# Routing of two expert mixtures in another order: loads, shift, masks, slots and ranking

## What is computed

```python
p_group = jax.nn.softmax((t @ w_rg + b_rg).astype(jnp.float32), axis=-1)
grp = jnp.argmax(p_group, axis=-1)
...
top_p, top_i = lax.top_k(jax.nn.softmax(logits_in, axis=-1), TOP_K)
top_p = top_p / jnp.sum(top_p, axis=-1, keepdims=True) * p_g
```

## Time and profile before

| what | value |
|---|---|
| timed runs | 1819.88, 1822.99, 1823.16 us; median 1822.99 |
| the profiled execution | 1820.98 us, its span 1819.2 us |
| busy in the span | TensorE 1633.8 us (90%), VectorE 553.0 us (30%), ScalarE 322.6 us (18%), POOL 174.0 us (10%) |
| chain that ended last | TensorE 70%, DMA 16%, VectorE 9% |
| first routing | norm's last sum ends at 779.05 us, first gather on TensorE at 808.54 us |
| second routing | last sum ends at 1272.7 us, first gather at 1296.86 us |

### The profile page before, as it was taken

The page is one execution under the profiler, slowest core; times in us unless marked ns, Lnnn a source line. Parts: engine busy times, 40 slices in busy tenths (PEclk is TensorE's granted clock), DMA queues, the critical chain, the costliest instruction groups (busy, mean ns, idle before and its releaser), DMA issues.

```text
span 1819.2 us, 21572 instructions
## 1 busy us (share of the span) xinstructions
PE 1633.8 (90%) x8392; PEld 1057.2 (58%) x8392; DVE 553.0 (30%) x1120; ACT 322.6 (18%) x648; POOL 174.0 (10%) x180
## 2 busy tenths in 40 slices
PE   5799999999999989969998789988799998999985
PEld 1466666776588868855554369757534543443433
DVE  2266666666520011153122110382511111011002
ACT  2223333333231100011001021241100000000001
POOL 1144333334300000000000000000000000000000
PEclk8799999999999978969999899899699999999999
DMA  9311110111834413418999974103299989999993
GB/s 392 145 52 46 35 46 27 43 46 35 337 114 162 142 67 123 147 54 349 421 421 420 421 278 161 48 1 120 88 409 422 395 349 422 421 359 387 421 422 158
DMA packets 59644, 404.91 MB, mean 223 GB/s; under 512 B 6782, under 2 KB 7938, under 8 KB 13232
## 3 DMA queue, kind: packets, MB, share of 16 engines
q1 hardware_dynamic: 53328, 381.92, 52.7%
q0 software_dynamic: 6240, 21.92, 4.0%
HBM read 402.71 MB, written 1.10 MB: 222 GB/s over the span
## 4 chain that ended last, share of the span: by engine, by line
PE 70%; DMA 16%; DVE 9%; issue 2%; ACT 1%; SPq 0%; DVEq 0%; POOL 0%; POOLq 0%; ACTq 0%
PE bank L601 69%; DMA ring<-in_moe 14%; DVE arena L1619 2%; DMA ring<-in_dense 2%; ACT arena L1261 1%; DVE arena L1650 1%; DVE arena L1666 1%; PE bank L1017 1%; DVE arena L1655 0%; DVE arena L1647 0%; DVE arena L1645 0%; DVE arena L1659 0%; DMA arena<-in_router_w 0%; DMA arena<-decay_rows 0%; DVE arena L1669 0%
## 5 line engine op out<-in xcount | busy, mean ns | idle before, releaser
L601 PE MATMUL bank<-ring,arena 128*64 128x512 f32 (+2 forms) x2304 | 521.5, 606 | 58.6 <-DMA ring<-in_moe 56.9
L601 PE MATMUL bank<-arena 128*128 128x128 f32 (+3 forms) x2864 | 426.5, 300 | 35.2 <-DVE arena L1949 14.6
L601 PEld LDWEIGHTS bank<-arena 128*128 128x128 f32 (+2 forms) x2864 | 379.0, 194 | 134.0 <-ACT arena L1261 47.8
L601 PEld LDWEIGHTS bank<-ring,arena 128*64 128x64 f32 (+2 forms) x2304 | 174.6, 138 | 369.9 <-issue 364.9
L1261 ACT ACTIVATE arena<-bank 128x256 f32<-128x256 f32 (+1 forms) x369 | 164.1, 451 | 1186.0 <-PE bank L601 892.1
L601 PE MATMUL bank<-hc,head_w 128*128 128x512 f32 (+1 forms) x384 | 166.3, 541 | 3.0 <-DMA head_w<-in_head_w 3.0
L1971 DVE TENSOR_TENSOR arena<-arena,bank 128x256 f32<-128x256 f32 x48 | 20.2, 422 | 360.7 <-ACT arena L1261 360.7
L601 PE MATMUL bank<-arena,ring 128*128 128x256 f32 x512 | 116.6, 388 | 4.3 <-ACT arena L1261 2.6
L601 PEld LDWEIGHTS bank<-arena,ring 128*128 128x128 f32 x512 | 99.7, 195 | 19.7 <-ACT arena L1261 3.4
L601 PE MATMUL bank<-hc,ring 128*128 128x256 f32 x512 | 110.7, 380 | 0.0
L601 PEld LDWEIGHTS bank<-hc,ring 128*128 128x128 f32 x512 | 97.5, 190 | 12.9
(11 more groups left out here) (241 smaller groups left out, 1056.7 us busy)
## 6 DMA issues: line engine op xcount, KB each, us to landing
ring<-in_moe SPq DMA_DIRECT2D x288, 1024.0 KB, 13.2
ring<-in_dense SPq DMA_DIRECT2D x72, 1024.0 KB, 7.0
head_w<-in_head_w POOLq DMA_DIRECT2D x27, 512.0 KB, 4.0
arena<-decay_rows POOLq DMA_DIRECT2D x16, 256.0 KB, 4.6
xc<-in_xc SPq DMA_DIRECT2D x1, 2048.0 KB, 8.6
arena<-bias_rows POOLq DMA_DIRECT2D x2, 1024.0 KB, 8.5
mats<-in_square SPq DMA_DIRECT2D x1, 1088.0 KB, 11.6
out_y<-xc SPq DMA_DIRECT2D x2, 512.0 KB, 2.9
```

Of the source, the lines that this page charges most:

```text
L601: return nc.tensor.matmul(out, lhsT, rhs_, start=start, stop=stop, **kw)
```

## The change

Both routings are changed in the same way:

- The router's weights and `attn` are loaded when the first of the eight residual tiles is there, not the last.
- VectorE only scales the tiles (one scalar-tensor-tensor each, with gain and norm), and ScalarE adds the shift (`shift`, an Identity with a bias column). TensorE adds the logits' bias first, not last; in the second routing this waits for the first shifted tile.
- The masks of the first and second choice that `route1` and `route2` already have are used for the slots; the gates' search for them goes. In the second routing `keep` is the sum of two masks, each multiplied by the chosen group.
- Slots are computed twice. `place_fixed` gives the fixed experts their slots, and all others a base of 4096, which no unit holds. The first gathers (two in the first mixture, one in the second) are made from it. Then the ranking runs, and `place_ranked` adds the ranked experts' bases, less 4096, and computes slots again. Counting and ordering come ahead of that in the first mixture, and last in the second.
- Constant tables (`make_tables`) are made before the logits come.

The diff, cut to its core (eight columns of indentation taken off where the code is inside `build`):

```diff
+FAR = 4096.0
...
-second = area(12480, QT, E1)
...
+base_fixed = area(16656, E1)
...
-    pool.wait_ge(s["residual"], KT)
+    pool.wait_ge(s["residual"], 1)
     pool.dma_start(arena[:, 10752:10752 + KT * (GROUPS1 + E1 + E2)], t["router_w"]).then_inc(s["router_landed"], 16)
     pool.dma_start(hw[:, 0:1024 + 4 * P], t["attn"]).then_inc(s["attn_landed"], 16)
...
-    pool.wait_ge(s["residual"], 3 * KT)
+    pool.wait_ge(s["residual"], 2 * KT + 1)
...
         logits = [bank[5][:, qt * width:(qt + 1) * width] for qt in range(QT)]
+        at = D + (0, GROUPS1 + E1)[m]
+        if m == 1:
+            pe.wait_ge(s["route_in"], KT + 1)
+        for qt in range(QT):
+            mm(logits[qt], ones[0:1, :], one_row[0:1, 0, at:at + width], qt == 0, False, skip_group_check=True)
         for k in range(KT):
-            pe.wait_ge(s[f"route_in{m}"], k + 1)
+            pe.wait_ge(s["route_in"], KT * m + k + 1)
             for qt in range(QT):
-                mm(logits[qt], src[:, k, qt * P:(qt + 1) * P], router_w[m][:, k, :], k == 0 and qt == 0, False,
-                   skip_group_check=True)
-        at = D + (0, GROUPS1 + E1)[m]
-        for qt in range(QT):
-            ins = mm(logits[qt], ones[0:1, :], one_row[0:1, 0, at:at + width], False, qt == QT - 1, skip_group_check=True)
+                ins = mm(logits[qt], src[:, k, qt * P:(qt + 1) * P], router_w[m][:, k, :], False,
+                         k == KT - 1 and qt == QT - 1, skip_group_check=True)
         ins.then_inc(s["logits_made"], 1)
...
+    def shift(m):
+        into = H if m == 0 else X
+        for k in range(KT):
+            by = mod[:, 3 * KT + k, 0:1] if m == 0 else V("ln1_b")[:, k:k + 1]
+            act.wait_ge(s["route_scaled"], KT * m + k + 1)
+            act_fn(into[:, k, :], into[:, k, :], ACT.Identity, bias=by).then_inc(s["route_in"], 1)
     def route(m, experts):
+        shift(m)
...
         ins = stt(X[:, j, :], bank[j % 4][:, 0:SEQ], mod[:, 2 * KT + j, 0:1], X[:, j, :], ALU.mult, ALU.add)
         ins.then_inc(s["residual"], 1)
     dve.wait_ge(s["rnorm"], 1)
-    for half in range(2):
-        ks_ = range(half * KT // 2, (half + 1) * KT // 2)
-        link(tt_(H[:, ks_[0]:ks_[-1] + 1, :], X[:, ks_[0]:ks_[-1] + 1, :], times(norm_r, len(ks_)), ALU.mult))
-        for k in ks_:
-            ts_(H[:, k, :], H[:, k, :], ffns[:, k:k + 1], mod[:, 3 * KT + k, 0:1], ALU.mult, ALU.add
-                ).then_inc(s["route_in0"], 1)
+    for k in range(KT):
+        stt(H[:, k, :], X[:, k, :], ffns[:, k:k + 1], norm_r, ALU.mult, ALU.mult).then_inc(s["route_scaled"], 1)
...
         return tt_(out, out, over(pick_m[:, 0:rows], c), ALU.is_equal)
-    def make_falling():
+    starts = rs[9]
+    def make_tables(m):
+        experts, first = (E1, E2)[m], FIXED[m]
         dve.wait_ge(s["attn_landed"], 16)
         link(ts_(falling, slot_numbers[:, 0:E1], -1.0, float(P), ALU.mult, ALU.add))
+        link(ts_(base_fixed[:, 0:first], slot_numbers[:, 0:first], float(CAP), None, ALU.mult))
+        link(nc.vector.memset(base_fixed[:, first:experts], FAR))
+        link(nc.vector.memset(base[:, 0:first], 0.0))
+        link(ts_(starts[:, 0:UNITS[m]], slot_numbers[:, 0:UNITS[m]], float(P), None, ALU.mult))
...
+            link(ts_(base[:, first:experts], free_[:, 0:n], float(CAP // 2), CAP * first - FAR, ALU.mult, ALU.add))
...
+            link(ts_(base[:, first:experts], free_[:, 0:n], float(CAP), CAP * first - FAR, ALU.mult, ALU.add))
...
-    def place_tokens(m, kept, gates):
+    def find_slots(m, first, second):
         experts = (E1, E2)[m]
-        first = rt[8][:, 0:QT * experts].rearrange("p (a b) -> p a b", a=QT)
-        prod = rt[9][:, 0:QT * experts].rearrange("p (a b) -> p a b", a=QT)
-        second_ = second[:, :, 0:experts]
-        top = rs[6][:, 0:QT]
-        link(red(choice_gates[:, 0, :], gates, AX_X, ALU.max))
-        link(first_largest(first, gates, choice_gates[:, 0, :], experts))
-        link(tt_(second_, kept, first, ALU.subtract))
-        link(tt_(prod, second_, gates, ALU.mult))
-        link(red(choice_gates[:, 1, :], prod, AX_X, ALU.add))
-        dve.wait_ge(s["placed"], m + 1)
+        prod = rt[8][:, 0:QT * experts].rearrange("p (a b) -> p a b", a=QT)
         place = position[:, :, 0:experts]
-        link(cp(counts_f[:, 0:experts], bank[6][:, 2 * experts:3 * experts]))
-        link(ts_(base[:, 0:FIXED[m]], slot_numbers[:, 0:FIXED[m]], float(CAP), None, ALU.mult))
-        link(cp(rt[0][:, 0:experts], counts_f[:, 0:experts]))
-        rank_experts(m, rt[0][:, 0:experts])
-        link(tt_(place, bank[6][:, 0:QT * experts].rearrange("p (a b) -> p a b", a=QT),
-                 times(base[:, 0:experts], QT), ALU.add))
         link(tt_(prod, place, first, ALU.mult))
         link(red(slot_of[:, 0:QT], prod, AX_X, ALU.add))
-        link(tt_(prod, place, second_, ALU.mult))
+        link(tt_(prod, place, second, ALU.mult))
         link(red(slot_of[:, QT:2 * QT], prod, AX_X, ALU.add))
-        starts = rs[9][:, 0:UNITS[m]]
-        link(ts_(starts, slot_numbers[:, 0:UNITS[m]], float(P), None, ALU.mult))
-        link(tt_(slot_in[:, :, 0:UNITS[m]], over(slot_of, UNITS[m]), times(starts, 2 * QT), ALU.subtract))
+        link(tt_(slot_in[:, :, 0:UNITS[m]], over(slot_of, UNITS[m]), times(starts[:, 0:UNITS[m]], 2 * QT), ALU.subtract))
+    def place_fixed(m, first, second):
+        experts = (E1, E2)[m]
+        dve.wait_ge(s["placed"], m + 1)
+        link(tt_(position[:, :, 0:experts], bank[6][:, 0:QT * experts].rearrange("p (a b) -> p a b", a=QT),
+                 times(base_fixed[:, 0:experts], QT), ALU.add))
+        link(cp(rt[0][:, 0:experts], bank[6][:, 2 * experts:3 * experts]))
+        find_slots(m, first, second)
+    def place_ranked(m, first, second):
+        experts = (E1, E2)[m]
+        place = position[:, :, 0:experts]
+        link(tt_(place, place, times(base[:, 0:experts], QT), ALU.add))
+        find_slots(m, first, second)
+    def choose_gates(m, second):
+        experts = (E1, E2)[m]
+        gates = gate_rows[:, :, 0:experts]
+        prod = rt[8][:, 0:QT * experts].rearrange("p (a b) -> p a b", a=QT)
+        link(red(choice_gates[:, 0, :], gates, AX_X, ALU.max))
+        link(tt_(prod, second, gates, ALU.mult))
+        link(red(choice_gates[:, 1, :], prod, AX_X, ALU.add))
...
+        link(cp(counts_f[:, 0:FIXED[m]], rt[0][:, 0:FIXED[m]]))
         link(red(top[:, 0:1], counts_f[:, 0:experts], AX_X, ALU.max))
         cp(most[:, :], top[:, 0:1]).then_inc(s["counted"], 1)
         order_experts(m)
...
-        place_tokens(0, keep[:, :, 0:E1], gate_rows[:, :, 0:E1])
+        place_fixed(0, top1, top2)
+        return top1, top2
...
-        link(tt_(w4, w4, top2, ALU.add))
         link(tt_(sm, m1, m2, ALU.add))
...
         link(tt_(w4, w4, over(hot, PER2), ALU.mult))
-        w3 = w.rearrange("p (a b) -> p a b", a=n)
-        cp(keep[:, :, 0:E2], w3).then_inc(s["kept"], 1)
+        link(tt_(top2, top2, over(hot, PER2), ALU.mult))
+        w3, top2_3 = (rt[i][:, 0:n * E2].rearrange("p (a b) -> p a b", a=n) for i in (3, 9))
+        tt_(keep[:, :, 0:E2], w3, top2_3, ALU.add).then_inc(s["kept"], 1)
         link(nc.vector.reciprocal(gm, gs))
         dve.wait_ge(s["kept"], 2)
-        link(tt_(w, w, ex, ALU.mult))
-        link(tt_(gate_rows[:, :, 0:E2], w3, over(gm, E2), ALU.mult))
-        place_tokens(1, keep[:, :, 0:E2], gate_rows[:, :, 0:E2])
-    def mixture(m):
+        link(tt_(ex3, ex3, keep[:, :, 0:E2], ALU.mult))
+        link(tt_(gate_rows[:, :, 0:E2], ex3, over(gm, E2), ALU.mult))
+        choose_gates(1, top2_3)
+        place_fixed(1, w3, top2_3)
+        return w3, top2_3
...
         make_gather(0)
+        if ahead == 2:
+            make_gather(1)
+        rank_experts(m, rt[0][:, 0:(E1, E2)[m]])
         copy_x(0)
-        make_gather(1)
+        if ahead == 2:
+            count_tokens(m)
+            choose_gates(m, second)
+        place_ranked(m, first, second)
+        if ahead == 1:
+            make_gather(1)
         for i, of in enumerate((slot_of, choice_gates.rearrange("p a b -> p (a b)"))):
             for j in range(2 * QT):
                 ins = ts_(slot_diag[:, 4 * i + j, :], M("ident"), of[:, j:j + 1], None, ALU.mult)
                 if i == 0 or j < 2 * QT - 1:
                     link(ins)
...
+            count_tokens(m)
         hidden(0)
...
+                stt(X[:, k, :], X[:, k, :], V(name + "_g")[:, k:k + 1], norm_r, ALU.mult, ALU.mult
+                    ).then_inc(s["route_scaled"], 1)
+            return
         for half in range(2):
             ks_ = range(half * KT // 2, (half + 1) * KT // 2)
             rows = X[:, ks_[0]:ks_[-1] + 1, :]
             link(tt_(rows, rows, times(norm_r, len(ks_)), ALU.mult))
```

More of the change, by code:

```diff
@@ L1858, in route1 @@
                 n = QT
-                make_falling()
+                make_tables(0)
                 dve.wait_ge(s["logits_made"], 1)
@@ L1989, in mixture @@
                 ins.then_inc(s["slots_spread"], 1)
```

(22 more changed lines are left out.)

5 lines of the change are left out of this document (2 added, 3 removed).

## The result

The changed kernel takes 1802.42 us (median of 5 runs, 1801.51 to 1808.37); beside it the kernel before took 1819.88 us (5 runs, 1816.44 to 1823.16). The ratio is 0.9917, its 95% interval 0.9896 to 0.9938: **0.83% faster**. The forecast was 1810 us, 0.65% off 1821.75. The five runs of before are the three that the forecast knew and two shorter ones, so their median fell from 1822.99 to 1819.88. The saving is thus 15.1 us by the ratio and 17.5 by the medians, where the sum had 11.8.

A forecast was written before the change was run, and what follows sets the result against it. Both expert mixtures were taken as bound by the weight stream, which stops during the routings. Gains of 3.1 + 5.3 + 0.7 + 2.65 = 11.8 us, taken from a mean of 1821.75, gave 1810 us, range 1803.5 to 1815.

The forecast's parts named there:

- Router weights in A, 3.1 us: First routing, up to the logits: earlier router start gains 2.13 us, bias moved into the pause 1.0; together 3.1 us.
- Logits to first gather, 5.3 and 2.65 us: Fixed slots ahead of the ranking start the first gather 5.3 us earlier in the first routing, 2.65 in the second.
- What lies in the gather's shadow: First routing: second gather and ranking, 4.7 us, hidden under TensorE's 6.75 us gather; slack 2.1, or 0.8 late at full clock.
- Slots, not the order: First mixture: the stream follows the release of slots, so it gains TensorE's shift of 8.4 us, not the restart's 12.
- About 856.5: First mixture, a sign: TensorE's first long wait for weights comes at about 856.5 us instead of 864.92.
- the restart at 815.2: First mixture: order at 811.3 us, plus 3.9 from order to moving weights, restarts the stream at 815.2.
- weights moving 4 us after the order: First mixture, a sign: the weight stream moves again 4 us after the ranked order is ready.
- No table load: ScalarE's Identity shifts cost no table load; the rival, chance 0.04, had 2 x 1.28 us more, 1812.6 us.
- the second routing's input, 0.7 us: Second routing: TensorE's router starts at 1274.88 instead of 1275.58 us; the bias stays in the chain; gain 0.7 us.
- the clock stays up: Rival, chance 0.20: shorter pauses keep TensorE's clock up, each routing's router passes gain up to 3.2 us more; 1803.6 us.
- the clock rises later: Rival, chance 0.07: the clock rises within `up` instead of before the gather's end, losing 3.5 us at most once; 1813.5 us.

The follow-up runs named there:

- late_loads: The changed kernel with the loads of router weights and table back at the last residual; 1806.16 us, ratio 0.9930.
- warm_more: The changed kernel with unread 256-column matmuls in TensorE's pauses of both routings (3, 4 and 7) and nine at the attention's start; 1795.12 us, ratio 0.9861; repeated 0.9852.
- order_late: The changed kernel with counting and ordering of the experts put back behind the diagonals in the first mixture; 1802.70 us, ratio 0.9920.
- inputs_only: The kernel before with the new input side alone (early loads, scaling and shift tile by tile, bias first); 1815.21 us, ratio 0.9977.
- masks_only: The kernel before with only the masks reused and the tables made earlier, the ranking still ahead of the first gather; 1813.51 us, ratio 0.9971.
- slots_only: The changed kernel with the input side of before (late loads, one wide multiplication, shifts by VectorE, bias last); 1806.31 us, ratio 0.9933.
- narrow: The changed kernel with three pauses of TensorE in each routing filled by six unread matmuls of 32 columns each; 1798.66 us, ratio 0.9900.

## Why the prediction was right, and where its sum was short

The mechanism came as forecast in A and in what follows the logits: the routing ends earlier, the first gather with it, and the stream of weights follows by slots. The two routings gave 16.05 us in the profiles where 11.8 were forecast. The missing 4.3 are 2.63 of the second routing's input beyond its 0.7, nearly all of it the router's clock, and 1.65 between the first gather matrices and `up`, where the gathers ran shorter. The time itself can't confirm the sum to better than this: the interval of the ratio, put on 1822.99, runs from 1804.0 to 1811.7.

- **Router weights in A, 3.1 us.** Measured 3.17 in the changed kernel, 3.16 alone. late_loads adds that the bias was bound to the same wait. Loads issued 27 us earlier cost nothing that shows: the stretch ahead of A took 772.98 to 777.80 us in the ten profiles with early loads and 777.19 to 778.56 in the four with late ones.
- **Logits to first gather, 5.3 and 2.65 us.** Measured 5.25 and 2.65. The new wait came where forecast, 0.79 us long. Inside the sum the masks carry more (1.91) and the ranking less than I had expected of the halves.
- **What lies in the gather's shadow.** It was covered, with 1.57 us to spare where I had worked out 2.1, because the gather itself became shorter. At the full clock the cover goes, as forecast, for 0.47 us (warm_more) where 0.8 were priced.
- **Slots, not the order.** The long wait for weights moved by 10.12 us, with the 10.49 of the first `up`; the hole came back at 822; order_late, with its order 4.8 us later, lost nothing. "About 856.5" was 854.80, since `up` moved by 10.49 and not by 8.4 (1.2 of it lie ahead of A).
- **A hit by chance: the restart at 815.2.** The rate was full from 815 to the hole at 822, but not for the reason given. The order came at 809.13, not at 811.3, and 3.9 us behind it would be 813.0; the sign "weights moving 4 us after the order" did not show. First weights moved at 810, before any ranked expert was needed, and the next loads waited for the end of `up` at 812.68 and not for the order. The 3.9 us hold where the order is what comes last: 811.15 to 815 in order_late.
- **No table load.** ScalarE's eight shifts in A took 3.31 us, 0.41 each, and nothing stands ahead of them but the wait for VectorE (the row is below). The Trainium skill (ScalarE: Activation LUTs, Table sets) says that identity is in every set; this trace agrees.
- **The term that was mis-sized: the second routing's input, 0.7 us, measured 3.33.** 0.64 us of it is what I had worked out (inputs_only). 2.27 are the router's 32 passes, 7.01 there and 4.74 in the changed kernel, and 0.42 the bias, 1.00 to 0.58: they now begin before the clock falls. This is the half of my rival "the clock stays up" that held, in one routing of two. In A the clock fell at 779.2, before the router's start at 779.92, so its passes kept their 7.04.
- **A term that was missing: the gathers.** They took 5.81 and 5.80 instead of 6.75 and 6.65, together 1.8 us. My rival "the clock rises later" had the sign wrong: what brought the rise inside the gathers forward no run isolates. A's gather took 6.55 us with the new input alone (inputs_only), 6.01 with the masks alone (masks_only) and 5.96 in slots_only, so in A it goes with VectorE's shorter chain ahead of the gather and not with the input.
- **The rival's second half.** I argued against it that eleven microseconds of such passes had not raised the clock. That holds for B of the kernel before (router, bias and transposes from 1275.58 to 1287.14, all at 0.50) and not for A: there the clock came back at 794 to 795, at the end of the same work (783.28 to 794.65), and fell again at 797 to 798, before the counts. A's counts thus ran at 1.2 GHz because the clock had fallen a second time, and filling the pauses with wide matmuls brought it back earlier and kept it up (warm_more), for another 7.4 us in the two routings. The Trainium skill (TensorE: Matmul & The Clock Gate, HAM oscillation) says that the array stays warm where its matmuls are not broken up by waits. The runs agree as far as the start goes: with the pause ahead of the router filled, the clock was still up there (narrow, 4.60 us). They do not agree further on: in `narrow` the clock fell at 782 to 783, when TensorE had been busy without a break since 780.

ScalarE's timeline of the changed kernel, to the point on the table load:

```profile
779.36 3.31 ACT L1264 ACTIVATE hc<-hc,mod 128x256 f32<-128x256 f32 x8 [0.55 <-DVE hc L1782]
```

**Open.** Why the clock fell when it did in B. After the end of the last variance sum, which took 3.72 us in both, it fell 2.0 us later in inputs_only and 5.3 in the changed kernel (5.3 in its second profile too). The next matmul came 2.25 us after that sum in both, so up to the first of the two falls TensorE had done the same:

```profile
1267.00:1268.00 1.00, 0.38 (x2) 0.41 (x3) 1.00 (x3) 1.00 (x3) 0.00 (x0) 0.70 0.00 0
1268.00:1269.00 1.00, 1.00 (x6) 0.96 (x6) 1.00 (x4) 1.00 (x4) 0.00 (x0) 0.50 0.00 0
```

These are inputs_only's windows; the changed kernel's stand in the result (0.96 at 1263). So 2.69 of the 16.05 us (17.04 - 14.35) are measured but not explained, and another kernel with this edit need not have them: late_loads has the new input side too, and its passes took 7.01 us in B. The attention's 3.2 us are unexplained as well.

## What to carry to other kernels

Ask of each operation in a serial stretch what it is needed for first. Here the first gather needed slots for the fixed experts only, and moving the rest behind it was worth 3.3 and 2.0 us, while having the order 4.8 us earlier was worth nothing, since slots held the stream. An early load pays for everything that is behind the same wait, so look what else stands there. And where TensorE goes through a chain of small matmuls, read the granted clock in windows of a microsecond before and behind each pause: filling three pauses in each routing with matmuls that nobody reads gave 7.4 us, nearly half as much as the whole change gave in the two routings (16.05).

## What was not expected of the hardware

The same 32 passes of 36 columns took 7.04 us in every profile whose clock had fallen before them and 4.50 to 4.60 in those where it fell within them. It fell there with TensorE busy all the time. The first gather's 32 passes took 3.81 at the full clock and 5.3 to 6.8 when the rise came inside. Narrow filling left the clock at 0.50 for 16 us in which TensorE was busy for 14.8; with wide filling in the same pauses it was back within two microseconds of the second filling's start (787.00, back at 788 to 789).
